# Two-layer mixer and mixture-of-experts block in fp32: the expert weights get another layout in DRAM

## The reference, cut to what matters

```python
N_GROUPS = 4; EXPERTS_PER_GROUP = 8; N_EXPERTS = 32; TOP_K = 2; D_EXPERT = 512

def hier_moe(h, w_group, b_group, w_expert, b_expert, w1, w3, w2):
    t, d = h.shape
    pg = jax.nn.softmax((h @ w_group) + b_group, axis=-1)
    g_prob, g_idx = lax.top_k(pg, 1)                       # one group of eight experts
    ...
    e_prob, e_idx = lax.top_k(jax.nn.softmax(le, axis=-1), TOP_K)   # two experts in it
    ...
    def expert_block(args):
        xb, e = args
        return (jax.nn.silu(xb @ w1[e]) * (xb @ w3[e])) @ w2[e]
    ...
```

## Time and profile before

| | |
|---|---|
| median of 3 runs | 4473.71 us (4470.65 to 4475.16) |
| the profiled execution | 4466.63 us, its span 4464.8 us |
| TensorE busy (matmul / weight load) | 3819.2 us (86%) / 2150.1 us |
| VectorE, ScalarE, GpSimd busy | 1545.7, 1355.4, 206.8 us |
| traffic | 697.62 MB in 454316 packets |
| of it the expert weights | 192 loads of 2048 KB, 403 MB |

### The profile page before, as it was taken

One profiled execution on the slowest core, in us unless ns is written; L12 is line 12 of the kernel. 1 busy time (PEld: TensorE's weight loads), 2 busy tenths in 40 slices (PEclk: granted clock), 3 DMA queues, 4 the chain that ended last, 5 costly groups with the idle time before them and its releaser, 6 DMA issues. The chain is left out here.

```text
span 4464.8 us, 76078 instructions
## 1 busy us (share of the span) xinstructions
PE 3819.2 (86%) x32246; PEld 2150.1 (48%) x32246; DVE 1545.7 (35%) x3747; ACT 1355.4 (30%) x2940; POOL 206.8 (5%) x199
## 2 busy tenths in 40 slices
PE   5999577777787699999898979989969988799997
PEld 2555366666666444666466543333335455233332
DVE  2000366666676112443236421111122183211112
ACT  2000234444433122332446422222225262222221
POOL 0000000000000000010110000000012000000000
PEclk7999789999999899999999989999979999899998
DMA  5221434343443220001210059999933000999997
GB/s 205 73 92 48 131 96 118 105 116 106 119 112 112 84 105 1 20 1 38 64 56 1 1 179 346 378 379 378 386 141 93 17 33 1 332 379 380 379 379 264
DMA packets 454316, 697.62 MB, mean 156 GB/s; under 512 B 169168, under 2 KB 195920, under 8 KB 453456
## 3 DMA queue, kind: packets, MB, share of 16 engines
q1 hardware_dynamic: 432752, 613.98, 40.0%
q0 software_dynamic: 14048, 53.49, 3.6%
q10 hardware_dynamic: 7168, 25.17, 1.4%
HBM read 625.72 MB, written 64.50 MB: 155 GB/s over the span
## 5 line engine op out<-in xcount | busy, mean ns | idle before, releaser
L200 PE MATMUL ps<-arena 128*128 128x384 f32 (+8 forms) x5516 | 1597.9, 454 | 183.2 <-issue 38.7
L200 PEld LDWEIGHTS ps<-arena 128*128 128x128 f32 (+4 forms) x5516 | 914.2, 192 | 834.6 <-issue 456.0
L2635 PE MATMUL ps<-arena 128*32 128x512 f32 x9216 | 1036.8, 603 | 50.1 <-DMA arena<-in_w 45.5
L2635 PEld LDWEIGHTS ps<-arena 128*32 128x32 f32 x9216 | 308.1, 111 | 681.0 <-issue 664.3
L576 PE MATMUL ps<-arena 64*64 64x64 f32 (+1 forms) x10624 | 459.3, 240 | 181.4 <-DVE arena L1137 65.3
L576 PEld LDWEIGHTS ps<-arena 64*64 64x64 f32 x10624 | 411.0, 145 | 260.8 <-issue 102.2
L2769 DVE COPY arena<-ps 128x384 f32<-128x384 f32 x64 | 35.7, 558 | 693.0 <-PE ps L2694 693.0
L206 PE MATMUL ps<-arena 128*128 128x128 f32 x1200 | 191.5, 295 | 82.6 <-DVE arena L3083 41.9
L2745 ACT ACTIVATE arena<-ps 96x512 f32<-96x512 f32 x64 | 38.0, 594 | 656.2 <-PE ps L2635 656.2
L206 PEld LDWEIGHTS ps<-arena 128*128 128x128 f32 x1200 | 145.6, 154 | 124.0 <-DVE arena L3083 45.3
L549 DVE SCALAR_TENSOR_TENSOR arena<-arena 128x768 f32<-128x768 f32 x48 | 45.1, 1012 | 353.3 <-PE ps L200 353.2
(11 more groups left out here) (281 smaller groups left out, 3618.8 us busy)
## 6 DMA issues: line engine op xcount, KB each, us to landing
arena<-in_w SPq DMA_DIRECT2D x192, 2048.0 KB, 22.6
arena<-in_w_mod SPq DMA_DIRECT2D x24, 2048.0 KB
arena<-in_mod_w SPq DMA_DIRECT2D x12, 2048.0 KB, 18.3
yb<-arena ACTq DMA_DIRECT2D x64, 384.0 KB, 6.3
arena<-in_rwkv_w_in SPq DMA_DIRECT2D x8, 2048.0 KB, 9.6
rkvg<-arena POOLq DMA_DIRECT2D x32, 384.0 KB, 2.6
arena<-rkvg SPq DMA_DIRECT2D x32, 384.0 KB, 3.8
arena<-di SPq DMA_DIRECT2D x192, 64.0 KB, 2.6
```

The source lines that it names most:

```text
L200: ins = pe.matmul(out, l, r, start=(i == 0), stop=(i == len(pairs) - 1))
L2635: return pe.matmul(bank[32 * at:32 * at + 32, :], left[:, k, 32 * g:32 * g + 32], right[:, k, :], start=first, stop=last)
```

## The change

On the host, each expert weight is laid out so that the 16 KB of one partition lie in one run: axis order (expert, partition, k, column), stored as an array of 32 x 128 x 4096. The load then reads [128 x 4096] from DRAM into the slot, whose bytes are the same as before. `MoreBlocks` gets the same edit. Nothing else is touched: the order of the loads, the ring, the waits and all work of the engines stay.

```diff
@@ ExpertBlocks.sp
-            name, n = (("w1", 512), ("w3", 512), ("w2", 1024))[w]
-            sp.dma_start(self.weight(i, w), kchunk(I[f"{name}_{l}"][i], 0, n)).then_inc(self.lands[q][0], 16)
+            name = ("w1", "w3", "w2")[w]
+            sp.dma_start(self.moe.slots[q % RING], I[f"{name}_{l}"][i]).then_inc(self.lands[q][0], 16)
@@ MoreBlocks.sp
-            sp.dma_start(self.weight(i, w), I[f"{name}_{l}"][bass.ds(experts[i], 1), :, :].rearrange("o (k p) n -> p (o k) n", p=128)
+            sp.dma_start(self.moe.slots[q % RING].unsqueeze(1), I[f"{name}_{l}"][bass.ds(experts[i], 1), :, :].rearrange("o p n -> p o n")
                          ).then_inc(self.landed(i, w)[0], 16)
@@ _layout (on the host)
         for n in ("w1", "w3", "w2"):
-            out[f"{n}_{l}"] = I[f"{n}_2"][l]
+            w = np.asarray(I[f"{n}_2"][l])
+            out[f"{n}_{l}"] = np.ascontiguousarray(w.reshape(32, -1, 128, w.shape[2]).transpose(0, 2, 1, 3)).reshape(32, 128, SLOT)
```

## The result

The changed kernel takes 4446.85 us in the median of 5 runs (4439.12 to 4449.08), and the kernel before beside it 4470.65 us. The ratio is 0.9947, with a 95% interval of 0.9933 to 0.9961: 17 to 30 us faster. The forecast was 4414, with a range of 4404 to 4442. The direction was right, and the gain is 40% of what was forecast.

What follows compares the result with a forecast made beforehand. Late DMA engines in the expert stages were taken as the bound: 61.8 us from a freed TensorE, less 2 for late loads and 0 for starts, gave 60 us, 4473.7 to 4414 us, range 4404 to 4442.

Steps and rivals of the forecast that it cites:

- What bounds the kernel: Both layers' expert stages: DMA engines are late, TensorE waits 45.5 us for weights; a free TensorE would give 61.8 us.
- Longer runs: Expert weight loads: 16 KB packets take 609 ns, 430 GB/s, the one term with a gain, all 61.8 us.
- the change doesn't do what it says: Weight loads cut into 2 KB packets, 4490, or time as before, 4474; slow side 0.08 together with Rival 2.
- Rival 2: Weight loads: long DRAM runs are slower, 4505 at 380 GB/s; chance 0.08 together with the other slow-side rival.
- The remaining 2.95 us: Expert blocks: 18.93 less 15.98 us for weights, put down to result store, row gather and what these disturb.
- P: Expert stages: time in which the DMA engines serve a block; forecast 17.58 us, all 61.8 us gained below 17.86.
- The rule for the end of the stage: Expert stages: ab(31) starts 3.0 + 28.67 P after ab(0)'s end, the queue taken as never empty.
- The starts: Layer starts: first gather up to 3.0 us earlier, but slowed 3 us by long packets; entered 0, 3 us either side.
- The later gathers and stores: Expert blocks: gathers and `yb` stores, landing after 8.0 and 6.3 us, take some 3 us more but cost nothing.
- rival 1: Weight loads: the rate stays at 4 KB's 410 GB/s, gain 39 us, 4435; chance 0.20 including rates of 410 to 422.
- no change: Whole kernel: time within 0.2% (9 us) of before, as if loads were limited by bytes in flight, 4474; chance 0.05.
- two signs of being wrong: Expert stages: weights alone under 420 GB/s, or a late gather or store queue making TensorE's waits change their name.

Runs made afterwards that it cites:

- run 5: On the changed kernel (16 KB runs), each gather fills 128 partitions in place of 96, the added rows unread: ratio 0.9884 to the kernel before.
- run 7: On the changed kernel, loads 4 to 7 of a layer wait until block 0's gather has landed: ratio 0.9930 to the kernel before.
- g128_16k_hold: On the changed kernel (16 KB runs), gathers of 128 rows plus loads 4 to 7 held back: ratio 0.9836 to the kernel before.

## Why the prediction was wrong, point by point

**What bounds the kernel: right.** The experts' stages, with the DMA engines late and a free TensorE at 17.04 us a block. The runs with 128-row gathers and long runs reached just that: 515.1 us from ab(0)'s end to ab(31) in layer 1, where 515.1 was worked out for a free TensorE, and 516.7 in layer 0.

**Longer runs: right in kind and size.** 434 GB/s for the weights alone where 430 was worked out, 616 ns for a packet where it was 609. "Long runs from DRAM are slower", "the rate stays at that of 4 KB" and "the change doesn't do what it says" all fall with that. Rival 2 feared streams that start 16 KB apart; with rows of 16 KB such a pitch leaves no gap, and a load reads one stretch of 2 MB.

**"The remaining 2.95 us": this step failed.** P = 6.291 / 0.430 + 2.95 took what the gather and the store cost over from the kernel before as a constant. It isn't one. With the weights at 14.63 us (14.50 at the measured 434 GB/s), the measured 18.23 leave 3.60 us (3.73). A gather puts six packets on each engine, and by turns about as many weight packets go beside them. Each lost 47 ns when it had 2 KB and 200 ns with 16 KB: 0.28 us for a block before and 1.20 now, 0.92 more. The gather's own packets got shorter in return: 221 ns over 2800 to 3000 us before (0.073 x 3200 us over the 1057 of 4.33 MB), 202 after, 0.11 us for a block. That makes some 0.8 us, against 0.65 to be explained, and run 5 shows that it is this: with 128 rows the loss went and TensorE ran free. The 0.65 us are nearly the whole miss in the steady part, for the limit was 17.86 and P had only 0.28 to spare. Of the 40 us that the profiled execution falls short of the 60 forecast, 30 are in the blocks (29.7 gained for 59.8), 8.3 in layer 1's start and 2 elsewhere. The sentence in the prediction that gathers disturb the loads, with 269 GB/s in the earlier trace rows, was the place to ask what this rate would be with long packets. I had put the price down to "what these disturb" and not asked what its unit was: it is paid by each weight packet beside a gather and grows with that packet's length, and isn't a fixed sum for each gather.

**The rule for the end of the stage: right but for an idle time.** By it P is 18.44 in layer 0, against 18.23 counted directly. After the change the first loads are through before ab(1) has freed the next slots, and the engines stand still, as these 4 us after show (2702 to 2706 us, 0.51 MB, nearly all of it in the first microsecond; the next packets come after 2706.4 us):

```profile
GB/s 492 1147 328 0 0 655 328 983 492 164 0 0 328 0 164 0 0 0 0 0 0 0 0 0 0 0 0 0 0 0 0 0 0 0 0 0 0 0 0 0
DMA packets 47, 0.51 MB, mean 127 GB/s; under 512 B 16, under 2 KB 16, under 8 KB 16
```

The rule took the queue as never empty, though faster loads empty it first. That is 28.67 x 0.21 = 6 us in layer 0 which weren't in the sum; this standstill is some 3 of them, and the rest stays open.

**The starts: right in layer 0; in layer 1 one of the two effects had the wrong sign.** Two effects were to cancel within 3 us. In layer 0 they did (ab(0) ends at 2689.30, before at 2689.58). In layer 1 the delay was 8.3 us. The alternation was counted for one gather's six packets only. But the stores of `htok` go by turns with the same loads. From 3812 to 3814 us, after:

```profile
q1 hardware_dynamic: 50, 0.79, 91.7%
q0 software_dynamic: 47, 0.16, 19.1%
```

So where the shorter loads were to let the first gather go up to 3 us earlier, in layer 1 it was issued 4.3 us later after the router (36.9 us, before 32.6): GpSimd waited 12.93 us for the stores (9.21 before). And the first gather took 11.5 us from issue to its use (7.5), 4.0 more, where 3 were counted: at a turn it waits for 812 ns and not 609, and 6 x (0.812 - 0.133) = 4.1 us. In run 7, which holds loads 4 to 7, both delays are gone.

**The later gathers and stores: right.** Their landings rose from 8.0 and 6.3 to 11.5 and 9.9 us, the 3 us that were said, and TensorE waited for none of the later gathers in the blocks. It was their cost on the engines that counted, not their own delay.

**The chances.** 4447 us fell between rival 1 (4422 to 4440, chance 0.20) and no change (0.05); that the gather's price would grow was on no list. Nor did the prediction's two signs of being wrong catch it: the weights alone ran at 434 GB/s, and TensorE's waits in the blocks kept their name and only shrank. Only block 0 of layer 1 waited longer for its gather. As a rival it would have read, with the loss since measured: P = 14.63 + 2.95 + 6 x (0.200 - 0.047) = 18.5 us, and 3 + 28.67 x 18.5 = 533.4 us for a layer's blocks, 27 us less than before in both.

What stays open is why 96 partitions are slow to fill. The store of `yb` reads 96 partitions and its packets aren't held up: 5.9% of 16 x 200 us over 1152 packets of 4 KB is 164 ns both in the kernel before and after. And a gather that runs alone, as it does where the loads are held, shows no such difference: 0.757 x 48 us / 161 = 226 ns for a 4 KB packet into 96 partitions (hold16k, 2656 to 2659 us, 0.66 MB), and 0.746 x 60.8 / 210 = 216 ns into 128 (g128_16k_hold, 2652 to 2655.8 us, 0.86 MB). The gap of 202 to 164 ns is one of gathers beside loads. The Trainium skill ("SBUF — State Buffer", "Door 1: The DMA port swizzle") has a rule that fits in part: partitions 0 to 63 are reached by half of the sixteen ports and 64 to 127 by the other half. With 96 rows, one half has eight rows on each port and the other four. As an estimate by that page, the gather's packets would take 8/6 of 160 ns (a 4 KB packet in the earlier trace rows), 213 ns; 205 were measured. The same page advises 128 partitions for a DMA-bound transfer ("The DMA setup-cost knee"); here they were worth 0.6% (0.9947 to 0.9884). No run varied which partitions are filled or how a transfer's rows are dealt out to the sixteen engines, and the 216 ns of the lone gather into 128 partitions don't follow from that rule, so the ports are an explanation and not shown.

## What to carry to other kernels

When a stream gets longer packets, look at what shares its engines: the queues take turns by packet, so everything else lands later, and a disturbance that is paid by each packet beside it grows with the packet. A "rest" that is left over when the main term is taken out of a period has a unit, and before it is carried over one should ask which of time, packets or bytes it is. A load into fewer than 128 partitions can slow the transfers beside it, as the gathers into 96 did here; filling the rest with rows nobody reads was faster than leaving them out.

## What the runs showed of the hardware that was not expected

- A load into 96 partitions, indirect or direct, takes 195 to 205 ns for a 4 KB packet on an engine beside the weight loads and brings their 16 KB packets from 616 to between 770 and 812 ns. With 128 partitions it is 176 and 626 ns. Which rows are read, the same one or others, makes no difference (809 ns for 812).
- A 16 KB packet is served whole: beside it a queue of 4 KB packets gets one packet for each, 111 to 111 in 6 us.
- SyncE needs 0.33 us to issue 2 MB in 128 runs of 16 KB and 0.37 in 256 of 8 KB (medians). With 2 and 4 KB runs it stood 4.75 us in the median though the quickest issue took 0.37; what it stood for, no run shows.
